# Two of three products of a split-precision matmul in one of 512 columns, in lane x's down and output projections

## The chip, the core and the metric

The kernel runs on one core of one Trainium2 chip. The metric is the time of one execution on the device in microseconds. A core has TensorE (PE in the profile; its weight loads are PEld), VectorE (DVE), ScalarE (ACT), GpSimd (POOL) and SyncE (SP), each with a queue of its own that runs in order, and DMA engines. Products land in PSUM, in eight banks of 128 partitions by 512 float32.

## The reference

Two blocks after each other, all float32, d_model 1024, 256 tokens of x and, in the second block, 256 tokens of a context. What matters is the shape of every layer of x:

```python
x = x + rms_norm(m, ln_mix_post[layer])           # m: a mixer, ends in "... @ w_out", 1024 -> 1024
h = rms_norm(x, ln_ffn_pre[layer])
x = x + rms_norm(swiglu(h, w_gate, w_up, w_down), ln_ffn_post[layer])   # w_down: 2816 -> 1024
```

x passes four mixers (pool/gating, sparse attention with retention, differential attention, grouped attention) and six feed-forward parts; so there are four output projections `@ w_out` and six down projections, each followed by an RMS norm of its result over the 1024 features. The context passes three feed-forward parts and one mixer beside it, as a second lane.

## The kernel before

Features lie on the partitions and tokens on the free axis: an activation is a stack of tiles of 128 features x 256 tokens (T = 256). Every matrix is read from HBM in blocks of 8 x 128 rows by 256 columns (1 MB; a down projection's first of three blocks has 6 x 128 rows). SP loads a block into one of four buffers `raw`, as soon as the block four before is done on TensorE.

**Three products for one.** The products must be nearly float32 but run in the faster type `f32r`. So each operand is split into an upper part, rounded to f32r, and the rest: W = whi + wlo, x = x_hi + x_lo. ACT writes whi (L223), DVE writes wlo in two halves (L230, L243). `three` (L267) then issues, for each of the k tiles of 128 inputs, whi x_hi, whi x_lo and wlo x_hi, all of 256 columns, into one half of a bank; all pass `product`, whose line is L264. Each product loads its 128x128 weights anew. `two_tiles` (L277) does a block: output tile m = 0, then m = 1; between them it emits whi and the first half of wlo for the block two or three further on (`splits`, L210), behind m = 1 the second half (`other_half`, L235). Split activations of lane x are `HNX_hi`, `HNX_lo` (8 tiles, the input of the in- and output projections) and `GX_hi`, `GX_lo` (22 tiles, the gated product, input of the down projection); each is a tensor of its own. Lane c, the context, has `HNC` and `GC`.

**Down projection** (in `ffn`, L419, lane x is the one that is not chunked): for each of four pairs of output tiles (mp), three blocks of 6, 8 and 8 k tiles, the two output tiles in two banks (`S.tiles`), of which half is used. **Output projection** (`linear`, L375, with `gain` given): four blocks, each two output tiles, two banks alike. After each pair `put_out` (L345) is emitted for the first and then the second tile: ACT reads the bank three times (L352 square, L355 square times gain, L356 copy times gain to `S.Y`), and DVE adds up (L366 and L368 the two sums of squares, L370 and L372 the product with the residual). The first tile waits for the semaphore `x_tile`, the second for the block. A bank is free for TensorE after the third ACT read.

**Behind it** `norm` (L588) sums over the partitions with small products (L538, first of `sumxy`, what L366 wrote), ACT takes the root (L525, after a table load L533), DVE inverts and spreads (L546), TensorE spreads over the partitions (L553), then DVE and ACT form the next HNX. Meanwhile TensorE gets work of lane c and of the modulation rows (L1115, L1129), as far as there is any.

**What sets the order.** All instructions are emitted by one Python program once per engine, so each engine's order is fixed. Generators for the lanes are stepped by a planner with estimated costs (`pace`, `fill`); its constants are not changed, so TensorE's order of blocks stays. Semaphore waits stand in the instruction streams: an engine waits and everything behind it waits too.

Of the kernel before, what the change touches and what calls it, by code (L numbers as in the profile page):

```python
# [9 lines left out]
P = 128  # L10
D = 1024
KD = D // P
T = 256
# [70 lines left out]
def build(nc, A, out):  # L84
# [4 lines left out]
    with ExitStack() as ctx:  # L89
        def sb(name, shape, dt=fp32):  # L90
            return ctx.enter_context(nc.sbuf_tensor(name, shape, dt))

        HX, HC = sb("HX", [P, KD, T]), sb("HC", [P, KD, T])
        WHI = [sb(f"whi{s}", [P, BLK], f32r) for s in range(HIS)]
# [5 lines left out]
        with ExitStack() as g:  # L100
            HNX = [g.enter_context(nc.sbuf_tensor(f"HNX_{n}", [P, KD, T], f32r)) for n in ("hi", "lo")]
            GX = [g.enter_context(nc.sbuf_tensor(f"GX_{n}", [P, KF, T], f32r)) for n in ("hi", "lo")]
        AX_HN, AX_G = 2 * KD * T, 2 * KF * T
# [4 lines left out]
        with ExitStack() as g:  # L108
# [21 lines left out]
        names += [f"{lane}_{n}" for lane in "xc" for n in (  # L130
            "evac", "tile", "tanh", "gate_read", "up_done", "g_hi", "g_lo", "sq", "sq_sum", "gg", "gg_sum", "hg", "hg_sum",
            "total", "root", "rstd", "scaled", "resid", "normed", "hn_hi", "hn_lo")]
# [42 lines left out]
        def program(pe=None, act=None, dve=None, pool=None, sp=None):  # L175
# [100 lines left out]

            def two_tiles(S, n, dsts, x, ks, start, stop, waits=None, signal=None, tiles=2, last=False):  # L277

                landed(n)
                for m in range(tiles):  # L280
                    mm = three(dsts[m], n, m * P, x, ks, start, stop, None if m else waits)
                    if mm is not None and m == 0 and signal is not None:
                        mm.then_inc(signal.sem, 1)
                    if m == 0:
                        splits(n, last, apart=True)
                    if m == 0 and tiles == 2:
                        opened[0] = S.tag
                        yield ("d",)
                    opened[0] = None
                other_half()  # L290
                if mm is not None:
                    mm.then_inc(sems["block_done"], 1)
# [20 lines left out]
            def halves(bank):  # L313
                return bank[:, 0:T], bank[:, T:2 * T]
# [28 lines left out]
            ALL = [(k, k) for k in range(KD)]  # L343

            def put_out(S, src, k, gain, *ready):  # L345

# [28 lines left out]
            def linear(S, name, blocks, dst, ready=(), first=None, gain=None):  # L375
# [10 lines left out]
                for j, (b, at, *alone) in enumerate(blocks):  # L386
                    tiles = 1 if alone else 2
                    if first is None or j >= 2:
                        yield ("D",)
                        n = take(S.tag, "w_main", base + b)  # L390
                        banks = (S.pair[j % 2], S.pair[j % 2])
                        dsts = halves(banks[0])
                        if gain is not None and not S.lag:
                            banks = S.tiles[2 * (j % 2)], S.tiles[2 * (j % 2) + 1]
                            dsts = banks[0][:, 0:T], banks[1][:, 0:T]
                        on(pe, *ready, *(free.get(x.name) for x in banks))
                        tile = up(f"{S.tag}_tile") if gain is not None else None
                        yield from two_tiles(S, n, dsts, S.HN, ALL, True, True, None, tile, tiles, gain is not None and j == len(blocks) - 1)
                        at_n = n
                    else:  # L400
                        banks, at_n, tile = (S.pair[j],) * 2, n + j, None

                    def job(banks=banks, at_n=at_n, at=at, tile=tile, tiles=tiles):
                        if gain is not None:
                            for m in range(2):
                                src = banks[m][:, 0:T] if not S.lag else halves(banks[m])[m]
                                free[banks[m].name] = put_out(S, src, at + m, gain, done(at_n) if m or S.lag else tile)
                            marks.append(free[banks[1].name])
                            return
# [9 lines left out]
            def ffn(S, which, gain, first):  # L419
# [6 lines left out]
                for c, pairs in enumerate(chunks):  # L426
                    for p in pairs:
# [30 lines left out]
                        def keep(p=p, nu=nu, kt=kt, down_done=down_done):  # L458
# [3 lines left out]
                            free[up_.name] = ud  # L462
                            g = [x[:, kt:kt + 2, :].rearrange("p a b -> p (a b)") for x in S.G]
                            if on(act, ud, down_done):
                                NS.activation(g[0], S.TMP[p % 2][:, :], ACT.Copy).then_inc(hi.sem, 1)  # L465
                            if on(dve, hi):
                                NV.tensor_tensor(g[1], S.TMP[p % 2][:, :], g[0].bitcast(fp32), SUB).then_inc(lo.sem, 1)
                            held[p % 2] = lo
# [6 lines left out]
                    if not S.chunked:  # L475
                        for mp in range(4):
                            banks = S.tiles[2 * (mp % 2)], S.tiles[2 * (mp % 2) + 1]
                            for cc, (k0, k1) in enumerate(SHORT_FIRST):
# [6 lines left out]
                                tile = up(f"{t}_tile") if cc == 2 else None  # L485
                                yield from two_tiles(S, n, [b[:, 0:T] for b in banks], S.G, ks, cc == 0, cc == 2, waits, tile, 2, mp == 3 and cc == 2)
                            for m in range(2):
                                free[banks[m].name] = put_out(S, banks[m][:, 0:T], 2 * mp + m, gain, done(n) if m else tile)
                        continue
# [1596 lines left out]
```

## Time and profile before

| | |
|---|---|
| time, median of 3 | 2722.41 us (2721.42 to 2722.43) |
| span of the profiled execution | 2725.8 us |
| TensorE products | 2528.6 us busy, 93% |
| TensorE weight loads | 2395.9 us, 88% |
| DVE | 1707.1 us, 63% |
| ACT | 1248.6 us, 46% |
| granted clock of TensorE | 0.97 of full speed on average |

A busy TensorE is read with care: its records overlap, so what counts is the distance from start to start. The page's slices say where it waits, the timeline what the wait was for. A mean duration is that of one record.

### The profile page before, as it was taken

What the parts mean: (1) busy time and instruction counts of PE and PEld (TensorE: products, weight loads), DVE (VectorE), ACT (ScalarE), POOL (GpSimd) and SP (SyncE); (2) the same over time, 40 slices, a digit from 0 to 9 for tenths busy, and PEclk for the clock granted to TensorE, in tenths of its full rate; (3) what the DMA queues carried; (4) which work ended last, traced back from release to release, by engine and by line L of the source; (5) the groups of instructions that cost most, each with busy time, mean ns of one, the idle gap of its engine ahead of it and who ended that gap; (6) DMA issues with size and microseconds to landing.
All of it is one profiled execution on the core that took longest, in us unless ns stands there. A gap on an engine that the chain in (4) does not pass through costs nothing.

```text
span 2725.8 us, 48854 instructions
## 1 busy us (share of the span) xinstructions
PE 2528.6 (93%) x20780; PEld 2395.9 (88%) x20780; DVE 1707.1 (63%) x2804; ACT 1248.6 (46%) x1697; POOL 1.2 (0%) x6
## 2 busy tenths in 40 slices
PE   6799997999999999999888998999999999887998
PEld 5689996888998999999887898999999999756997
DVE  6565574656766565566767576577655557646655
ACT  4443453444544444445445554455444345435443
POOL 0000000000000000000000000000000000000000
PEclk9899999999999999999898999999999999888999
DMA  6456656533555665544351344555545555363453
GB/s 218 181 200 242 241 203 229 189 109 124 186 202 216 236 226 196 211 147 154 132 174 52 120 171 154 185 175 173 179 170 179 180 177 183 114 215 137 170 178 116
DMA packets 71591, 480.14 MB, mean 176 GB/s; under 512 B 8784, under 2 KB 9296, under 8 KB 17744
## 3 DMA queue, kind: packets, MB, share of 16 engines
q1 hardware_dynamic: 66240, 468.74, 48.8%
q10 hardware_dynamic: 5136, 8.28, 1.0%
q8 instruction: 166, 2.72, 0.4%
q14 instruction: 49, 0.40, 0.0%
HBM read 471.48 MB, written 1.05 MB: 173 GB/s over the span
## 4 chain that ended last, share of the span: by engine, by line
PE 73%; DVE 13%; ACT 7%; DMA 4%; issue 3%; ACTq 0%; DVEq 0%
PE bank L264 64%; ACT whi L223 4%; DVE wlo L243 2%; DMA raw<-w_main 2%; DVE wlo L230 2%; PE bank L1115 2%; DMA raw<-w_down 1%; PE bank L997 1%; PE bank L935 1%; DVE ARX L686 1%; DVE HX L637 1%; DVE tmpx L631 1%; PE bank L985 1%; PE bank L553 0%; PE bank L1639 0%
## 5 line engine op out<-in xcount | busy, mean ns | idle before, releaser
L264 PE MATMUL bank<-HNX_hi,whi 128*128 128x256 f32 x2968 | 866.2, 293 | 64.3 <-DVE wlo L243 24.4
L223 ACT ACTIVATE whi<-raw 128x2048 fp32r<-128x2048 f32 (+1 forms) x378 | 705.5, 1868 | 334.6 <-PE bank L264 149.4
L264 PE MATMUL bank<-HNX_hi,wlo 128*128 128x256 f32 x2968 | 849.8, 287 | 0.0
L264 PE MATMUL bank<-HNX_lo,whi 128*128 128x256 f32 x2968 | 834.6, 286 | 0.0
L230 DVE TENSOR_TENSOR wlo<-raw,whi 128x1024 fp32r<-128x1024 f32 (+1 forms) x378 | 453.4, 1199 | 570.1 <-ACT whi L223 569.5
L264 PEld LDWEIGHTS bank<-HNX_hi,whi 128*128 128x128 f32 x2968 | 582.4, 196 | 91.7 <-issue 50.7
L264 PEld LDWEIGHTS bank<-HNX_hi,wlo 128*128 128x128 f32 x2968 | 583.1, 196 | 0.0
L264 PEld LDWEIGHTS bank<-HNX_lo,whi 128*128 128x128 f32 x2968 | 573.2, 196 | 1.1 <-issue 0.9
L243 DVE TENSOR_TENSOR wlo<-raw,whi 128x1024 fp32r<-128x1024 f32 (+1 forms) x378 | 450.8, 1193 | 0.0
L264 PE MATMUL bank<-HNC_hi,whi 128*128 128x256 f32 x1344 | 390.2, 290 | 11.6 <-DVE tmpc L448 4.5
L264 PE MATMUL bank<-HNC_lo,whi 128*128 128x256 f32 x1344 | 381.7, 284 | 0.0
L264 PE MATMUL bank<-HNC_hi,wlo 128*128 128x256 f32 x1344 | 381.6, 284 | 0.0
L264 PE MATMUL bank<-GX_hi,whi 128*128 128x256 f32 x1056 | 302.6, 287 | 4.0 <-DVE wlo L243 3.9
L264 PE MATMUL bank<-GX_lo,whi 128*128 128x256 f32 x1056 | 298.7, 283 | 0.0
L264 PE MATMUL bank<-GX_hi,wlo 128*128 128x256 f32 x1056 | 298.6, 283 | 0.0
L264 PEld LDWEIGHTS bank<-HNC_hi,whi 128*128 128x128 f32 x1344 | 259.2, 193 | 22.5 <-issue 7.9
L264 PEld LDWEIGHTS bank<-HNC_lo,whi 128*128 128x128 f32 x1344 | 259.4, 193 | 0.6 <-issue 0.2
L264 PEld LDWEIGHTS bank<-HNC_hi,wlo 128*128 128x128 f32 x1344 | 259.2, 193 | 0.0
L264 PEld LDWEIGHTS bank<-GX_hi,whi 128*128 128x128 f32 x1056 | 202.4, 192 | 10.4 <-DVE wlo L243 7.8
L264 PEld LDWEIGHTS bank<-GX_lo,whi 128*128 128x128 f32 x1056 | 202.5, 192 | 0.1
L264 PEld LDWEIGHTS bank<-GX_hi,wlo 128*128 128x128 f32 x1056 | 202.4, 192 | 0.0
L465 ACT ACTIVATE GX_hi<-tmpx 128x512 fp32r<-128x512 f32 x66 | 41.7, 632 | 250.0 <-DVE tmpx L461 250.0
(349 smaller groups left out, 2923.7 us busy)
## 6 DMA issues: line engine op xcount, KB each, us to landing
raw<-w_main SPq DMA_DIRECT2D x270, 1024.0 KB, 4.8
raw<-w_ada SPq DMA_DIRECT2D x72, 1024.0 KB, 4.8
raw<-w_down SPq DMA_DIRECT2D x72, 1024.0 KB, 4.9
raw<-w_down SPq DMA_DIRECT2D x36, 768.0 KB, 4.2
raw<-w_cmp SPq DMA_DIRECT2D x4, 1024.0 KB, 4.8
tmpx<-ARX ACTq DMA_DIRECT2D x18, 128.0 KB, 4.8
tmpx<-ARX ACTq DMA_DIRECT2D x32, 64.0 KB, 4.7
HX<-x_in SPq DMA_DIRECT2D x2, 512.0 KB, 6.0
```

What stands on the lines that cost most here:

```text
L223: NS.activation(WHI[q % HIS][:, 0:size], RAW[m % SLOTS][:, 0:size], ACT.Copy).then_inc(sems["w_hi"], 1)
L230: NV.tensor_tensor(WLO[m % SLOTS][:, 0:half], RAW[m % SLOTS][:, 0:half], WHI[q % HIS][:, 0:half].bitcast(fp32), SUB)
L243: NV.tensor_tensor(WLO[m % SLOTS][:, half:size], RAW[m % SLOTS][:, half:size], WHI[q % HIS][:, half:size].bitcast(fp32), SUB).then_inc(sem ...
L264: return NT.matmul(dst, (WHI[ordinal[n] % HIS], WLO[n % SLOTS])[w][:, k * 2 * P + col:k * 2 * P + col + P], x[xp][:, kx, :], start=start, ...
L465: NS.activation(g[0], S.TMP[p % 2][:, :], ACT.Copy).then_inc(hi.sem, 1)
L631: NV.tensor_tensor(S.TMP[k % 2][:, 0:T], S.Y[:, k, :], S.wide_y[:, 0:T], MUL).then_inc(sc.sem, 1)
L637: NV.tensor_tensor(S.H[:, k, :], S.H[:, k, :], S.TMP[k % 2][:, 0:T], ADD).then_inc(re.sem, 1)
L686: NV.scalar_tensor_tensor(S.Y[:, k, :], S.H[:, k, :], gain(k), S.wide_h[:, 0:T], MUL, MUL).then_inc(no.sem, 1)
L935: mm = NT.matmul(bank[:, c0 + c * T:c0 + (c + 1) * T], q[pr, :], k[pr, :], start=True, stop=True)
L985: mm = NT.transpose(turn_bank[:, c * P:(c + 1) * P], PB[w % 3][:, 0, c * P:(c + 1) * P], ident)
L997: mm = NT.matmul(out_bank[:, 0:P], v, PT[b][:, c * P:(c + 1) * P], start=c == 0, stop=c == len(vs) - 1)
L1115: mm = NT.matmul(bank[32 * g:32 * g + 32, 0:T], CCOL[:, k, 6 - 2 * r:38 - 2 * r], RAW[n % SLOTS][:, k * T:(k + 1) * T], start=r == 0 and k ...
```

## The change

In the down and output projections of lane x, `by_sides` takes the place of `three`: the upper weights are multiplied with x_hi and x_lo, which now lie side by side in one tensor (`HNX`, `GX` of shape [128, k, 2, 256]), in one product of 512 columns over a whole bank, and the lower weights with x_hi in one of 256 columns into the bank's first half. The bank then holds two partial results. A new function `both_sides` has DVE add the two halves, with a reduction over pairs, into half of `TMP[1]` (two places, by turns), and `put_out` reads from there instead of from the bank. A bank is free after that reduction. A new semaphore `x_added` orders reduction and readers; the reduction also waits until the readers of two tiles before are done. The other products of lane x (input projections, gate and up) and lane c keep three products. Where the split activations are written, the access patterns become strided over the two parts.

```diff
--- before.py
+++ after.py
@@ -90,6 +90,9 @@
         def sb(name, shape, dt=fp32):
             return ctx.enter_context(nc.sbuf_tensor(name, shape, dt))
 
+        def parts(pair):
+            return pair[:, :, 0, :], pair[:, :, 1, :], pair
+
         HX, HC = sb("HX", [P, KD, T]), sb("HC", [P, KD, T])
         WHI = [sb(f"whi{s}", [P, BLK], f32r) for s in range(HIS)]
 
@@ -98,8 +101,8 @@
         WLO = [sb(f"wlo{s}", [P, BLK], f32r) for s in range(SLOTS)]
 
         with ExitStack() as g:
-            HNX = [g.enter_context(nc.sbuf_tensor(f"HNX_{n}", [P, KD, T], f32r)) for n in ("hi", "lo")]
-            GX = [g.enter_context(nc.sbuf_tensor(f"GX_{n}", [P, KF, T], f32r)) for n in ("hi", "lo")]
+            HNX = parts(g.enter_context(nc.sbuf_tensor("HNX", [P, KD, 2, T], f32r)))
+            GX = parts(g.enter_context(nc.sbuf_tensor("GX", [P, KF, 2, T], f32r)))
         AX_HN, AX_G = 2 * KD * T, 2 * KF * T
         ARX = sb("ARX", [P, AX_HN + AX_G + KD * T])
         YX = ARX[:, AX_HN + AX_G:AX_HN + AX_G + KD * T].rearrange("p (a b) -> p a b", a=KD)
@@ -128,7 +131,7 @@
         names = ["w_in0", "w_in1", "w_in2", "w_in3", "w_hi", "w_lo", "block_done", "ada_out", "gain",
                  "in_h0", "in_h1", "in_ctx", "in_vec", "in_tab", "act_c", "pe_step", "act_step", "dve_step", "pool_step", "swapped0", "swapped1", "stored"]
         names += [f"{lane}_{n}" for lane in "xc" for n in (
-            "evac", "tile", "tanh", "gate_read", "up_done", "g_hi", "g_lo", "sq", "sq_sum", "gg", "gg_sum", "hg", "hg_sum",
+            "evac", "tile", "added", "tanh", "gate_read", "up_done", "g_hi", "g_lo", "sq", "sq_sum", "gg", "gg_sum", "hg", "hg_sum",
             "total", "root", "rstd", "scaled", "resid", "normed", "hn_hi", "hn_lo")]
         for n in names:
             sems[n] = ctx.enter_context(nc.semaphore(n))
@@ -274,11 +277,21 @@
                                          stop and j == len(ks) - 1 and w == 1)
                 return mm
 
-            def two_tiles(S, n, dsts, x, ks, start, stop, waits=None, signal=None, tiles=2, last=False):
+            def by_sides(bank, n, col, x, ks, start, stop, waits=None):
+
+                mm = None
+                for j, (k, kx) in enumerate(ks):
+                    if on(pe, *(waits or {}).get(kx, ())):
+                        NT.matmul(bank[:, :], WHI[ordinal[n] % HIS][:, k * 2 * P + col:k * 2 * P + col + P],
+                                  x[2][:, kx, :, :].rearrange("p a b -> p (a b)"), start=start and j == 0, stop=False)
+                        mm = product(bank[:, 0:T], n, col, k, x, 0, kx, 1, False, stop and j == len(ks) - 1)
+                return mm
+
+            def two_tiles(S, n, dsts, x, ks, start, stop, waits=None, signal=None, tiles=2, last=False, sides=False):
 
                 landed(n)
                 for m in range(tiles):
-                    mm = three(dsts[m], n, m * P, x, ks, start, stop, None if m else waits)
+                    mm = (by_sides if sides else three)(dsts[m], n, m * P, x, ks, start, stop, None if m else waits)
                     if mm is not None and m == 0 and signal is not None:
                         mm.then_inc(signal.sem, 1)
                     if m == 0:
@@ -341,6 +354,15 @@
                 splits(n + 1)
 
             ALL = [(k, k) for k in range(KD)]
+
+            def both_sides(S, bank, k, *ready):
+
+                at = k % 2 * T
+                added = up(f"{S.tag}_added")
+                if on(dve, *ready, free.get((S.tag, "added", k % 2))):
+                    NV.tensor_reduce(S.TMP[1][:, at:at + T], bank[:, :].rearrange("p (s t) -> p t s", s=2), AX, ADD).then_inc(added.sem, 1)
+                free[bank.name] = added
+                return S.TMP[1][:, at:at + T], added
 
             def put_out(S, src, k, gain, *ready):
 
@@ -391,11 +413,11 @@
                         banks = (S.pair[j % 2], S.pair[j % 2])
                         dsts = halves(banks[0])
                         if gain is not None and not S.lag:
-                            banks = S.tiles[2 * (j % 2)], S.tiles[2 * (j % 2) + 1]
-                            dsts = banks[0][:, 0:T], banks[1][:, 0:T]
+                            dsts = banks = S.tiles[2 * (j % 2)], S.tiles[2 * (j % 2) + 1]
                         on(pe, *ready, *(free.get(x.name) for x in banks))
                         tile = up(f"{S.tag}_tile") if gain is not None else None
-                        yield from two_tiles(S, n, dsts, S.HN, ALL, True, True, None, tile, tiles, gain is not None and j == len(blocks) - 1)
+                        yield from two_tiles(S, n, dsts, S.HN, ALL, True, True, None, tile, tiles, gain is not None and j == len(blocks) - 1,
+                                             gain is not None and not S.lag)
                         at_n = n
                     else:
                         banks, at_n, tile = (S.pair[j],) * 2, n + j, None
@@ -403,9 +425,12 @@
                     def job(banks=banks, at_n=at_n, at=at, tile=tile, tiles=tiles):
                         if gain is not None:
                             for m in range(2):
-                                src = banks[m][:, 0:T] if not S.lag else halves(banks[m])[m]
-                                free[banks[m].name] = put_out(S, src, at + m, gain, done(at_n) if m or S.lag else tile)
-                            marks.append(free[banks[1].name])
+                                if S.lag:
+                                    free[banks[m].name] = ev = put_out(S, halves(banks[m])[m], at + m, gain, done(at_n))
+                                    continue
+                                src, added = both_sides(S, banks[m], at + m, done(at_n) if m else tile)
+                                free[S.tag, "added", m] = ev = put_out(S, src, at + m, gain, added)
+                            marks.append(ev)
                             return
                         ev = up(f"{S.tag}_evac")
                         if on(act, done(at_n), *free.get((S.tag, "dst"), ())):
@@ -460,11 +485,11 @@
                             if on(dve, done(nu), held["read", p % 2]):
                                 NV.scalar_tensor_tensor(S.TMP[p % 2][:, :], S.TMP[p % 2][:, :], 0.5, up_[:, :], MUL, MUL).then_inc(ud.sem, 1)
                             free[up_.name] = ud
-                            g = [x[:, kt:kt + 2, :].rearrange("p a b -> p (a b)") for x in S.G]
+                            g, both = [x[:, kt:kt + 2, :] for x in S.G[:2]], S.TMP[p % 2][:, :].rearrange("p (a b) -> p a b", a=2)
                             if on(act, ud, down_done):
-                                NS.activation(g[0], S.TMP[p % 2][:, :], ACT.Copy).then_inc(hi.sem, 1)
+                                NS.activation(g[0], both, ACT.Copy).then_inc(hi.sem, 1)
                             if on(dve, hi):
-                                NV.tensor_tensor(g[1], S.TMP[p % 2][:, :], g[0].bitcast(fp32), SUB).then_inc(lo.sem, 1)
+                                NV.tensor_tensor(g[1], both, g[0].bitcast(fp32), SUB).then_inc(lo.sem, 1)
                             held[p % 2] = lo
                             lo_marks[kt // 2] = lo
                         after(S, keep)
@@ -483,9 +508,10 @@
                                 ks = [(k - k0, k) for k in range(k0, k1)]
                                 waits = {k: [lo_marks[k // 2]] for k in range(k0, k1) if k % 2 == 0} if mp == 0 else None
                                 tile = up(f"{t}_tile") if cc == 2 else None
-                                yield from two_tiles(S, n, [b[:, 0:T] for b in banks], S.G, ks, cc == 0, cc == 2, waits, tile, 2, mp == 3 and cc == 2)
+                                yield from two_tiles(S, n, banks, S.G, ks, cc == 0, cc == 2, waits, tile, 2, mp == 3 and cc == 2, True)
                             for m in range(2):
-                                free[banks[m].name] = put_out(S, banks[m][:, 0:T], 2 * mp + m, gain, done(n) if m else tile)
+                                src, added = both_sides(S, banks[m], 2 * mp + m, done(n) if m else tile)
+                                free[t, "added", m] = put_out(S, src, 2 * mp + m, gain, added)
                         continue
                     k0, k1 = CHUNKS[c]
                     for mp in range(4):
```

## Rows read from the trace of the kernel before

**Rows 1.** The page, parts 1 and 4: busy time by engine, and the chain by line.
```profile
PE 2528.6 (93%) x20780; PEld 2395.9 (88%) x20780; DVE 1707.1 (63%) x2804; ACT 1248.6 (46%) x1697; POOL 1.2 (0%) x6
...
PE bank L264 64%; ACT whi L223 4%; DVE wlo L243 2%; DMA raw<-w_main 2%; DVE wlo L230 2%; PE bank L1115 2%; DMA raw<-w_down 1%; PE bank L997 1%; PE bank L935 1%; DVE ARX L686 1%; DVE HX L637 1%; DVE tmpx L631 1%; PE bank L985 1%; PE bank L553 0%; PE bank L1639 0%
```

**Rows 2.** Groups, part 5: busy us, mean ns, idle before.
```profile
L264 PE MATMUL bank<-GX_hi,whi 128*128 128x256 f32 x1056 | 302.6, 287 | 4.0 <-DVE wlo L243 3.9
```

**Rows 3.** Timeline, TensorE, full clock: start us, duration us, instruction, count.
```profile
355.15 0.28 PE L264 MATMUL bank<-GX_hi,whi 128*128 128x256 f32 x1
355.27 0.28 PE L264 MATMUL bank<-GX_lo,whi 128*128 128x256 f32 x1
```

**Rows 4.** Timeline, TensorE, half clock.
```profile
1312.26 0.41 PE L264 MATMUL bank<-HNX_hi,whi 128*128 128x256 f32 x1
1312.47 0.41 PE L264 MATMUL bank<-HNX_hi,wlo 128*128 128x256 f32 x1
```

**Rows 5.** Timeline, TensorE, full clock, float32; first row is the second's first record.
```profile
673.34 0.59 PE L818 MATMUL bank<-tmpx,VEC 128*128 128x512 f32 x1
673.34 1.02 PE L818 MATMUL bank<-tmpx,VEC 128*128 128x512 f32 x2
...
1448.01 0.27 PE L985 MATMUL bank<-VEC,ARX 128*128 128x128 f32 x1
1448.12 0.61 PE L997 MATMUL bank<-ARX 128*128 128x128 f32 x4
```

**Rows 6.** Groups of DVE, shapes apart.
```profile
L961 DVE TENSOR_REDUCE SMALL<-bank 128x1 f32<-128x512 f32 x48 | 31.5, 685 | 15.5 <-PE bank L935 15.5
...
L1436 DVE TENSOR_TENSOR ARX<-ARX 64x480 f32<-64x480 f32 x4 | 3.9, 963 | 1.0 <-PE bank L1448 0.9
...
L575 DVE TENSOR_REDUCE diagx<-ARX 128x256 f32<-128x1024 f32 x1 | 1.9, 1880 | 0.0
```

**Rows 7.** Timeline, ACT, output projection of the last mixer.
```profile
2485.84 1.92 ACT L223 ACTIVATE whi<-raw 128x2048 fp32r<-128x2048 f32 x1
...
2491.79 0.38 ACT L352 ACTIVATE sqx<-bank 128x256 f32<-128x256 f32 x1 [1.77 <-PE bank L264]
...
2492.43 0.48 ACT L356 ACTIVATE ARX<-bank,GA 128x256 f32<-128x256 f32 x1
...
2499.06 1.92 ACT L223 ACTIVATE whi<-raw 128x2048 fp32r<-128x2048 f32 x1
```

**Rows 8.** Timeline, DVE, ends of two output projections.
```profile
713.79 0.42 DVE L366 TENSOR_TENSOR sumxy<-sumxy,sqx 128x256 f32<-128x256 f32 x1
...
2506.50 0.42 DVE L366 TENSOR_TENSOR sumxy<-sumxy,sqx 128x256 f32<-128x256 f32 x1
...
2507.96 0.42 DVE L366 TENSOR_TENSOR sumxy<-sumxy,sqx 128x256 f32<-128x256 f32 x1
```

**Rows 9.** Timeline, TensorE, first total at stage ends; bracket: idle before, releaser.
```profile
364.60 0.32 PE L538 MATMUL bank<-sumxy,VEC 128*32 128x64 f32 x8
...
718.80 0.32 PE L538 MATMUL bank<-sumxy,VEC 128*32 128x64 f32 x8
...
1302.74 0.44 PE L538 MATMUL bank<-sumxy,VEC 128*32 128x64 f32 x8 [3.47 <-DVE sumxy L366]
...
2315.67 0.32 PE L538 MATMUL bank<-sumxy,VEC 128*32 128x64 f32 x8 [1.25 <-DVE sumxy L366]
...
2508.43 0.44 PE L538 MATMUL bank<-sumxy,VEC 128*32 128x64 f32 x8 [3.63 <-DVE sumxy L366]
...
2712.73 0.32 PE L538 MATMUL bank<-sumxy,VEC 128*32 128x64 f32 x8 [1.25 <-DVE sumxy L366]
```

**Rows 10.** Timeline, ACT, after the first output projection.
```profile
118.46 1.28 ACT L533 ACT_TABLE_LOAD   x1
...
122.09 1.91 ACT L223 ACTIVATE whi<-raw 128x2048 fp32r<-128x2048 f32 x1 [2.13 <-DMA raw<-w_main]
123.90 0.30 ACT L525 ACTIVATE sqx<-bank,VEC 128x64 f32<-128x64 f32 x1
```

## The prediction

> **What bounds the kernel now.** I read the page's totals and chain first. TensorE is busy 93% of the span and one line, the split-precision product L264, is 64% of the chain that ended last [rows 1]. So a nanosecond off a product is a real nanosecond wherever TensorE streams without a gap. The grouped view then gives the part touched: 1056 products of each kind on GX [rows 2], and by the loops another 4 x 8 x 8 = 256 on HNX in the four output projections: 1312 triples. The timeline of TensorE shows their pitch: one product every 0.120 us at full clock [rows 3]. Last I read what TensorE waits for where a stage ends: L538 adds up the sums of `put_out`, and there the reader should look at the brackets [rows 9]. In five of the ten stage ends of x it comes without a wait, after work of lane c; in the other five something of the sums or the ACT queue behind them comes last. In those, TensorE's speed does not set the end; the DVE/ACT chain does.
>
> **The triple.** Old cost 3 x 0.120 = 0.360 us. New: one product of 512 columns and one of 256; as many columns, one weight load fewer. The second keeps 0.120. What the first costs no row shows. At half clock the same 256-column product has a pitch of 0.21 us [rows 4], which is 256/1.2 GHz = 0.213 with nothing on top; at full clock 0.120 stands against 256/2.4 = 0.107, so 0.013 us is on top. Three readings. (a) The load limits it and hides under a longer stream: the float32 records of 512 columns, at two clocks per column, come 1.02 - 0.59 = 0.43 apart = 2 x 0.213 with no excess [rows 5], so 0.213 + 0.120 = 0.333, say 0.336. (b) It is a cost of each product: 0.227 + 0.120 = 0.347. (c) It is a limit of the rate at which this type streams, and the half clock hides it: 0.240 + 0.120 = 0.360, no gain. Against (a): with a fresh load of 128 columns each, float32 records of 128 columns (as many clocks, at two per column) keep a pitch of (0.61 - 0.27)/3 = 0.113 [rows 5], so a load need not take 0.120. I take (b), between the ends and nearest to the row of the product itself: 0.013 saved per triple, 2.35 us in a down projection (176 triples), 0.85 in an output projection (64), 17.5 us in all, if nothing else intervened. The ends are 31.5 us and 0.
>
> The Trainium skill, TensorE: Matmul & The Clock Gate, section Back-to-back issue gap, gives a warm gap of N/2.4 + 2.5 ns: 216 ns for 512 columns, which is reading (a). By that rule the total above would be 31.5 us; but the same rule gives 109 ns for 256 columns and the trace shows 120, so it misses just the term in dispute.
>
> **The added reduction.** 80 times (10 stages x 8 tiles) DVE reads 512 elements of a bank in pairs 256 apart and writes 256. A contiguous reduction of 512 from a bank takes 0.685 us; two operations on SBUF that step over elements are dearer, 1.880 us for 1024 and 0.963 for 480 [rows 6], a slope of 0.917/544 = 1.69 ns per element and 0.15 fixed. That gives 0.15 + 512 x 0.00169 = 1.02 us. Ends: 0.69 (a bank does not mind the step) and 1.4 (if the cost were per output of the reduction). I take 1.02, the row with the same access order. DVE as a whole has room; the total of 80 us is not the price.
>
> The Trainium skill speaks against this edit: SBUF — State Buffer, section Door 1: The DMA port swizzle, says PSUM lines hold two FP32 values and non-contiguous patterns cost; VectorE: DVE Perf Modes, in its table of TRN2 errata, has 120 + FD cycles for a bank source, 0.66 us here, 0.36 less than my term. The sum by it would be some 8 us lower.
>
> **The added order.** This costs more. Before, ACT read the bank directly, so it ran its three operations of tile k+1 (1.12 us from start to end, [rows 7]) while DVE still added those of tile k; DVE needs 1.46 us per tile [rows 8] (from one last L366 to the next). Now DVE must reduce tile k+1 before ACT may start, and that reduction stands in DVE's queue behind the four adds of tile k, of which the last two wait for ACT. So DVE holds 1.02 + 1.12 + 0.9 (two adds) = 3.05 us per tile, 1.6 more. Behind it in DVE's queue are the halves of wlo; behind ACT's part is the next whi (1.92 us, [rows 7]).
> In a down projection a pair of tiles has three weight blocks (15 us of TensorE) for 6.1 us of this and 6.5 us of wlo: hidden. In an output projection each pair has one block: whi 1.9, wlo 2.35 (two halves of 1.2), first tile 3.05, second until ACT is free 2.1, together 9.4 us per block against 5.5 us of TensorE. Now the whi of two blocks apart come at 2485.84 and 2499.06, 6.6 per block [rows 7]. Blocks are split two ahead, so TensorE is not held inside; the lag comes out at the end.
>
> **Stage by stage, against the profiled execution.**
> - Output projection ending at 2508.43 (nothing covers it, TensorE already waits 3.63 us on L366 [rows 9]): whi slips from 2499.06 [rows 7] to 2506.0 (1.4 in the first block, 2.8 in each of two); then whi 1.9, a short copy of ACT 0.4, second whi 1.9, wlo 2.35, put_out of both tiles to the last L366 3.05 + 1.91 = 11.5, so 2517.5: **+9.1**.
> - The one ending at 118.54: there ACT's L525 comes only at 123.90, since a whi before it waits for its DMA until 122.09 [rows 10]; that is 5 us of cover. The last ACT operation of put_out now ends where the table load L533 starts, at 118.46 [rows 10]; the lag puts it 6.3 later (about 1 after the first block, 2.8 after each of the next two, nothing in the last, which splits no block), to 124.8; then table load 1.3, whi 1.9 and L525 at 128.0: **+4.1**.
> - The one ending at 718.80: L366 ends at 714.21 [rows 8] and TensorE comes 4.6 us later [rows 9]. The lag, with two whi in the last block as at 2508, is 9.1 again and brings L366 to 723.3: **+4.5**. The third output projection (at 1631) has lane c between its blocks, so the lag is smaller, and it too is covered: **-0.9**.
> - Down projections at 364.60 and two like it, where TensorE comes without a wait [rows 9] and the chain is 3.1 longer: **-2.35 each, -7.0**.
> - At 1302.74, waiting 3.47 us [rows 9], with wlo just before: 3.05 - 2.35 = **+0.7**. At 2315.67: the first tile's reduction waits for wlo, the last L366 comes 2.4 later: **0**. At 2712.73: 1.25 later: **-1.1**.
>
> Sum +9.3 us. Banks come free earlier or as before (the reduction ends before the old third ACT read). The strided writes to HNX/GX and the fewer instructions I take at nothing: same element counts. 2725.8 of span stands for a median of 2722.4, 3.4 more; 2735.1 of span is **2731.7 us**.
>
> **Rivals.**
> - *Load hidden, cheap reduction (faster).* Reading (a) and 0.69 us: (a) gives back 12 us more where TensorE sets the pace (6 x 1.9 + 0.7), the cheaper reduction 8 us in the exposed ends (6 to 8 of them in a row at 118, 718 and 2508). 2731.7 - 20 = 2711.5. For: no excess in the 0.43 row. Against: the 0.113 row and both stepping rows. Chance 0.20.
> - *Load hidden, reduction at 1.02:* 2731.7 - 12 = 2719.7, within 0.2%. Chance 0.21.
> - *Rate limit (slower).* Reading (c): the six down projections gain nothing, 15 us more: 2746.7. For: half clock hides the excess wholly, as a rate limit would. It decides from a 512-column pitch of 0.235 up. Chance 0.24.
> - *The change does what it says and DVE's order costs more* (splits of lane c late behind x's longer chain at 718 and after): 5 to 10 us on top of any case; I have no row for it, it widens the upper end.
> - *Forecast:* 0.35, own range 2724 to 2741, of which the lower tenth is within 0.2%.
>
> 0.2% is 5.4 us, about what a measurement can tell from no change. Faster 0.21 (the first rival and an edge), same 0.26, slower 0.53. The range leaves out half of the first rival and the worst of the third with late splits: 2710 to 2750.
>
> **What would show it.** Right: L264 on GX with 128x512 at a pitch near 0.227; reductions near 1.0 us; L538 at the ends of both uncovered output projections waiting 8 us and more on DVE's L366, whi blocks 9 us apart in them; the down projections about 2.3 us shorter. Wrong: a pitch of 0.215 or 0.24; a reduction near 0.7; output projections whose last L366 keeps its distance to the last product, which would mean that I misread the order of DVE's queue.

## The result and the profile after

The changed kernel takes 2781.22 us (median of 4, 2779.68 to 2789.38) where the kernel before takes 2722.42 on the same chip; ratio 1.0232, interval 1.0219 to 1.0244. It is slower by 59 us, and the forecast was 2731.7, at most 2750. The profiled execution has a span of 2787.3 us, 61.5 more than that of before; the table below accounts for those. It is the slowest of the four executions.

The page of the changed kernel, parts 1 and 5 (busy us, share, count; then groups: busy us, mean ns, idle before and its releasers):

```profile
PE 2538.4 (91%) x19468; PEld 2337.1 (84%) x19468; DVE 1766.9 (63%) x2884; ACT 1255.0 (45%) x1697; POOL 1.2 (0%) x6
...
L285 PE MATMUL bank<-GX,whi 128*128 128x512 f32 x1056 | 385.7, 407 | 14.0 <-DVE wlo L246 14.0
...
L363 DVE TENSOR_REDUCE tmpx<-bank 128x256 f32<-128x512 f32 x80 | 54.8, 685 | 15.6 <-PE bank L267 15.6
```

The busy shares have hardly moved against [rows 1]. The reduction took 0.685 us, as the contiguous one of [rows 6] does. The first totals of lane x's stage ends, for [rows 9] (timeline of TensorE; the bracket is its idle time and who ended it):

```profile
125.32 0.44 PE L564 MATMUL bank<-sumxy,VEC 128*32 128x64 f32 x8 [3.23 <-DVE sumxy L388]
370.90 0.32 PE L564 MATMUL bank<-sumxy,VEC 128*32 128x64 f32 x8
738.07 0.32 PE L564 MATMUL bank<-sumxy,VEC 128*32 128x64 f32 x8
1026.40 0.32 PE L564 MATMUL bank<-sumxy,VEC 128*32 128x64 f32 x8
1340.52 0.44 PE L564 MATMUL bank<-sumxy,VEC 128*32 128x64 f32 x8 [6.37 <-DVE sumxy L388]
1668.01 0.32 PE L564 MATMUL bank<-sumxy,VEC 128*32 128x64 f32 x8
1994.73 0.32 PE L564 MATMUL bank<-sumxy,VEC 128*32 128x64 f32 x8
2371.32 0.44 PE L564 MATMUL bank<-sumxy,VEC 128*32 128x64 f32 x8 [3.23 <-DVE sumxy L388]
2570.10 0.44 PE L564 MATMUL bank<-sumxy,VEC 128*32 128x64 f32 x8 [8.45 <-DVE sumxy L388]
2774.28 0.32 PE L564 MATMUL bank<-sumxy,VEC 128*32 128x64 f32 x8 [2.07 <-DVE sumxy L388]
```

Set against the same marks before, how much longer each stretch up to its mark became:

| mark before | what ends there | forecast | measured |
|---|---|---|---|
| 118.54 | output projection | +4.1 | +6.8 |
| 364.60 | down projection | -2.35 | -0.5 |
| 718.80 | output projection | +4.5 | +13.0 |
| 1008.21 | down projection | -2.35 | -1.1 |
| 1302.74 | down projection | +0.7 | +19.6 |
| 1630.95 | output projection | -0.9 | -0.7 |
| 1947.08 | down projection | -2.35 | +10.6 |
| 2315.67 | down projection | 0 | +8.0 |
| 2508.43 | output projection | +9.1 | +6.0 |
| 2712.73 | down projection | -1.1 | -0.1 |

Four stretches (718, 1302, 1947, 2315) hold 51 of the 61 us. The two that I had called certain losses at their ends (118 and 2508) make 12.8 where 13.2 was forecast. All the brackets of TensorE's timeline together are 187.0 us before and 239.3 after: 52.3 us of new waiting. The pitch gives some 9 back (below), so by difference about 18 us are left for running at the lower clock. The timeline gives the same when it is counted: at the lower clock the distances from start to start exceed those of the same shapes at full clock by 59.7 us in all before and by 79.0 after. The mean granted clock fell from 0.966 to 0.956. Here TensorE comes back from 3.00 us of waiting at 1.2 GHz, with a pitch of 0.21 us like that of [rows 4], and keeps it for 5.8 us.

```profile
377.65 0.58 PE L267 MATMUL bank<-HNC_hi,whi 128*128 128x256 f32 x1 [3.00 <-DVE tmpc L473]
378.03 0.42 PE L267 MATMUL bank<-HNC_lo,whi 128*128 128x256 f32 x1
378.25 0.42 PE L267 MATMUL bank<-HNC_hi,wlo 128*128 128x256 f32 x1
```

That block of lane c began 3.1 us later, counted from the stage end before it, and finished another 2.4 later. So this wait cost more than its bracket.

**Where the 19.6 us come from.** Between the blocks of the down projection at 1302, lane c computes its attention: small products, read by ACT (L1058, now L1084), and TensorE's next small product waits for that read. First a place in the kernel before, ACT and then DVE (timeline):

```profile
1240.05 0.39 ACT L352 ACTIVATE sumxy<-bank 128x256 f32<-128x256 f32 x1
...
1242.00 1.98 ACT L223 ACTIVATE whi<-raw 128x2048 fp32r<-128x2048 f32 x1
1243.81 0.44 ACT L1058 ACTIVATE ARC<-bank 128x256 f32<-128x256 f32 x1
```
```profile
1240.69 0.49 DVE L1050 SCALAR_TENSOR_TENSOR ARC<-ARC,SMALL 128x256 f32<-128x256 f32 x1
1241.09 1.22 DVE L243 TENSOR_TENSOR wlo<-raw,whi 128x1024 fp32r<-128x1024 f32 x1
1242.22 0.42 DVE L361 TENSOR_TENSOR sumxg<-HX,ARX 128x256 f32<-128x256 f32 x1
```

The same place in the changed kernel, DVE, ACT, and TensorE behind them:

```profile
1261.20 1.22 DVE L246 TENSOR_TENSOR wlo<-raw,whi 128x1024 fp32r<-128x1024 f32 x1
1262.33 0.68 DVE L363 TENSOR_REDUCE tmpx<-bank 128x256 f32<-128x512 f32 x1
1264.30 0.42 DVE L383 TENSOR_TENSOR sumxg<-HX,ARX 128x256 f32<-128x256 f32 x1 [1.28 <-ACT ARX L378]
1264.64 0.68 DVE L363 TENSOR_REDUCE tmpx<-bank 128x256 f32<-128x512 f32 x1
1265.81 0.43 DVE L388 TENSOR_TENSOR sumxy<-sumxy,sqx 128x256 f32<-128x256 f32 x1 [0.48 <-ACT sqx L374]
```
```profile
1263.05 0.42 ACT L374 ACTIVATE sumxy<-tmpx 128x256 f32<-128x256 f32 x1 [2.78 <-DVE tmpx L363]
...
1265.36 0.42 ACT L374 ACTIVATE sqx<-tmpx 128x256 f32<-128x256 f32 x1 [1.09 <-DVE tmpx L363]
...
1266.48 1.89 ACT L226 ACTIVATE whi<-raw 128x2048 fp32r<-128x2048 f32 x1
1268.28 0.36 ACT L1084 ACTIVATE ARC<-bank 128x256 f32<-128x256 f32 x1
```
```profile
1269.00 1.23 PE L1045 MATMUL bank<-KC,ARC 64*128 64x256 f32 x4 [3.77 <-ACT ARC L1084]
```

Before, ACT began its six reads of the banks at 1240.05, before DVE had even come to the half of wlo (1241.09). Now it begins only behind that half and a reduction. From the start of the same half of wlo, ACT's first read went from 1.04 us ahead to 1.85 behind, that is 2.9 us; and from that first read to whi it takes 3.43 us instead of 1.95, since ACT waits 1.09 for the second reduction, which stands behind DVE's 1.28 for ACT. Both together put the read L1084 4.4 us later against that half of wlo, and TensorE waits 3.77 for it, where the timeline of before shows no wait. DVE isn't full: it waits too. Two engines with room hand each tile to and fro, and a third one waits behind both. The same wait comes again at 1294.3 and 1318.6, with brackets of 4.32 and 4.29. The group of these small products, before and then changed:

```profile
L1019 PE MATMUL bank<-KC,ARC 64*128 64x256 f32 x64 | 11.2, 426 | 4.3 <-ACT ARC L1058 4.3
```
```profile
L1045 PE MATMUL bank<-KC,ARC 64*128 64x256 f32 x64 | 11.8, 444 | 14.7 <-ACT ARC L1084 14.7
```

Of the 15.5 us of new brackets in this stretch that is 10.4; the wait at its end holds another 2.9 (6.37 against 3.47).

**The stretches to 1947 and 2315 have another wait.** These small products stand in the stretch to 1302 alone. In the other two, lane c's norm and the split weights come late behind x's chain. TensorE, before and then changed: the largest wait inside x's down projection in the stretch to 1947, then that for lane c's norm in the stretch to 2315.

```profile
1899.38 0.38 PE L264 MATMUL bank<-GX_hi,whi 128*128 128x256 f32 x1 [0.77 <-DVE wlo L243]
2304.66 0.48 PE L553 MATMUL bank<-tmpc,VEC 128*128 128x256 f32 x1 [0.31 <-DVE tmpc L546]
```
```profile
1945.16 0.80 PE L285 MATMUL bank<-GX,whi 128*128 128x512 f32 x1 [4.12 <-DVE wlo L246]
2357.18 0.79 PE L579 MATMUL bank<-tmpc,VEC 128*128 128x256 f32 x1 [2.76 <-DVE tmpc L572]
```

Over the whole kernel the waits of TensorE for wlo are the largest part of the 52.3 us, 20.6 of them (waits of TensorE, before and then changed: us in total, times, longest):

```profile
PE bank L264 <- DVE wlo L243: 28.6, 24, 3.5
```
```profile
PE bank L267 <- DVE wlo L246: 30.0, 19, 4.2
...
PE bank L285 <- DVE wlo L246: 19.2, 14, 4.1
```

### The profile page after: what moved, and what is told of

It reads as the page before. It is cut to its first block, busy times and chain, and to the rows that moved or that the text cites. A ratio compares the mean times of both kernels' runs of the same rounds, so it can differ in the third digit from the quotient of the medians.

```text
span 2787.3 us, 46388 instructions
## 1 busy us (share of the span) xinstructions
PE 2538.4 (91%) x19468; PEld 2337.1 (84%) x19468; DVE 1766.9 (63%) x2884; ACT 1255.0 (45%) x1697; POOL 1.2 (0%) x6
## 4 chain that ended last, share of the span: by engine, by line
PE 64%; DVE 17%; ACT 10%; issue 4%; DMA 4%; ACTq 0%; DVEq 0%
PE bank L267 50%; PE bank L285 6%; ACT whi L226 5%; DVE wlo L246 3%; DMA raw<-w_main 3%; DVE wlo L233 3%; PE bank L1141 2%; DVE tmpx L363 1%; PE bank L1023 1%; ACT diagx L377 1%; PE bank L961 1%; ACT ARX L378 1%; DMA raw<-w_down 1%; DVE ARX L712 1%; DVE HX L663 1%
## 5 line engine op out<-in xcount | busy, mean ns | idle before, releaser
L267 PE MATMUL bank<-HNX,whi 128*128 128x256 f32 x5424 | 1023.9, 290 | 63.3 <-DVE wlo L246 25.6
L267 PEld LDWEIGHTS bank<-HNX,whi 128*128 128x128 f32 x5424 | 868.3, 196 | 89.3 <-issue 48.3
L267 PE MATMUL bank<-HNX,wlo 128*128 128x256 f32 x2968 | 848.7, 287 | 0.0
L267 PEld LDWEIGHTS bank<-HNX,wlo 128*128 128x128 f32 x2968 | 582.0, 196 | 0.0
L285 PE MATMUL bank<-GX,whi 128*128 128x512 f32 x1056 | 385.7, 407 | 14.0 <-DVE wlo L246 14.0
L267 PE MATMUL bank<-GX,wlo 128*128 128x256 f32 x1056 | 299.1, 283 | 0.0
L285 PEld LDWEIGHTS bank<-GX,whi 128*128 128x128 f32 x1056 | 202.3, 192 | 68.6 <-DVE wlo L246 18.2
L267 PEld LDWEIGHTS bank<-GX,wlo 128*128 128x128 f32 x1056 | 203.2, 192 | 0.1
L267 PE MATMUL bank<-GC_hi,whi 128*128 128x256 f32 x528 | 155.1, 294 | 4.3 <-DVE wlo L246 4.3
L267 PE MATMUL bank<-GC_lo,whi 128*128 128x256 f32 x528 | 150.9, 286 | 0.0
```

The source lines that it names most:

```text
L267: return NT.matmul(dst, (WHI[ordinal[n] % HIS], WLO[n % SLOTS])[w][:, k * 2 * P + col:k * 2 * P + col + P], x[xp][:, kx, :], start=start, ...
L285: NT.matmul(bank[:, :], WHI[ordinal[n] % HIS][:, k * 2 * P + col:k * 2 * P + col + P], x[2][:, kx, :, :].rearrange("p a b -> p (a b)"), st ...
```

## The experiments

The kernel before ran in the same rounds; times are medians, and ratios are to it. Three theories: A, the passing of each tile between DVE and ACT; B, DVE's added work; C, the wide product or what belongs to it.

**Without the addition.**
```diff
-src, added = both_sides(S, banks[m], 2 * mp + m, done(n) if m else tile)
-free[t, "added", m] = put_out(S, src, 2 * mp + m, gain, added)
+free[banks[m].name] = put_out(S, banks[m][:, 0:T], 2 * mp + m, gain, done(n) if m else tile)
```


> The products as changed, but no reduction: put_out reads the first side of the bank with ACT as before; whi x_lo is computed and not added in the four output and six down projections, so the result lacks that part. Theory A (order): the loss comes from DVE and ACT having to pass each tile to and fro; the products themselves gain 1312 x (0.360 - 0.353) = 9.2 us: 2713 us. Theory B (DVE time): the 80 x 0.685 = 55 us of reductions crowd DVE; also 2713. Theory C (product): the 512-column product, the full bank or the strided split activations cost elsewhere; then it stays near the changed kernel, 2770 or more.


Measured 2712.69 against 2719.85, ratio 0.9977 (0.9967 to 0.9987). C falls: wide products, full banks and strided activations are no loss but a gain of some 7 us (3.5 to 9.0 by the interval), a little under the pitch's 9.2. The brackets of TensorE are 187.8 us, as before the change (187.0): the new waiting comes with the addition.

**Narrow products, with the addition.**
```diff
-NT.matmul(bank[:, :], WHI[...], x[2][:, kx, :, :]..., start=start and j == 0, stop=False)
+product(bank[:, 0:T], n, col, k, x, 0, kx, 0, start and j == 0, False, True)
+product(bank[:, T:2 * T], n, col, k, x, 1, kx, 0, False, False, True)
```


> Two sides and the reduction, but three products of 256 columns as before (whi x_lo goes to the second side on its own). A and B: the changed kernel's time plus the 9.2 us that the pitch of 0.353 gave: 2790 us. C: the loss goes with the wide product, 2725 to 2740.


Measured 2787.43, ratio 1.0249 (1.0234 to 1.0263). The whole loss comes without a single wide product.

**A reduction that nobody reads.** DVE reduces 512 elements of HX at the same places, 680 ns each, and `put_out` reads the bank.
```diff
-NV.tensor_reduce(S.TMP[1][:, at:at + T], bank[:, :].rearrange("p (s t) -> p t s", s=2), AX, ADD).then_inc(added.sem, 1)
+NV.tensor_reduce(S.TMP[1][:, at:at + T], S.H[:, 0:2, :].rearrange("p a b -> p (a b)").rearrange("p (t s) -> p t s", s=2), AX, ADD)
```


> As the first, and a reduction of 512 to 256 elements stands in DVE's queue at the same places behind the same waits on TensorE, but reads the residual stream and nobody waits for it; ACT reads the bank directly. The result lacks whi x_lo as there. Theory A: DVE has room, and what costs is that ACT waits for DVE; so most of the loss is gone, 2713 plus 0.7 to 1.4 in each of the five uncovered stage ends, some 2720 (2714 to 2730). Theory B: nearly the whole loss is there, 2765 to 2785.


Measured 2722.97, ratio 1.0007 (0.9997 to 1.0016): 10 us above the kernel without addition (8 by the ratios). B alone is worth that, of the 68 us (69 by the ratios) that lie between the kernel without addition and the changed one.

**A wait without a reduction.**
```diff
+NV.tensor_reduce(S.TMP[1][:, at:at + 1], S.H[:, 0, 0:2], AX, ADD).then_inc(added.sem, 1)
+gate = both_sides(S, 2 * mp + m, done(n) if m else tile)
+free[banks[m].name] = free[t, "added", m] = put_out(S, banks[m][:, 0:T], 2 * mp + m, gain, gate)
```


> In the changed kernel's order, but in place of the reduction DVE does one element (two numbers of the residual stream into one, a cost of next to nothing), for which ACT waits before it reads the first side of the bank itself; the sum with whi x_lo is left out. It prices the waits alone. Theory A (the passing to and fro): of the 68 us between the kernel without addition (2713) and the changed one (2781) more than half stays without any reduction: 2748 to 2765. Rival (the reduction's own 0.69 us, in DVE's queue and in the chain, is the price): 2715 to 2730.


Measured 2745.64, ratio 1.0085 (1.0066 to 1.0103). The operation it adds takes 0.15 us (DVE, groups):

```profile
L362 DVE TENSOR_REDUCE tmpx<-HX 128x1 f32<-128x2 f32 x80 | 11.9, 149 | 23.7 <-PE bank L267 23.7
```

33 of the 68 us (29 of 69 by the ratios), slightly below the range of A and far above the rival's: ACT standing behind DVE's queue costs three times what the reductions cost as work. Work alone 10, wait alone 33, both 68: the other 25 to 32 come only together. I have not split these further, and their cause stays open. One reason may be that the reduction's own time now stands in the chain twice per pair. Another may be that ACT's three reads take longer from `TMP` than from the bank: 1.12 us from tile to tile (1241.83 to 1242.95 below) against 0.97 before (1240.05 to 1241.02).

**Both reductions ahead of both `put_out`.**
```diff
+sums = [both_sides(S, banks[m], 2 * mp + m, done(n) if m else tile) for m in range(2)]
 for m in range(2):
-    src, added = both_sides(S, banks[m], 2 * mp + m, done(n) if m else tile)
-    free[t, "added", m] = put_out(S, src, 2 * mp + m, gain, added)
+    free[t, "added", m] = put_out(S, sums[m][0], 2 * mp + m, gain, sums[m][1])
```


> The changed kernel with the two reductions of a pair of tiles emitted ahead of both put_out. Theory A: worked from the changed kernel's timeline (reductions 0.69, three reads of ACT 1.2, four adds 1.46), ACT is then held about 3.1 us per pair instead of 4.0 to 4.7 and DVE 4.4 instead of 5.6, so a third to a half of the 60 us goes: 2750 us (2740 to 2762). Theory B: DVE's work is the same, 2778 to 2783.


Measured 2748.74, ratio 1.0100 (1.0085 to 1.0115): the same operations in another order are 32 us cheaper (36 by the ratios). At the place above ACT now runs its six reads in one go:

```profile
1241.83 0.42 ACT L374 ACTIVATE sumxy<-tmpx 128x256 f32<-128x256 f32 x1 [2.78 <-DVE tmpx L363]
1242.15 0.49 ACT L377 ACTIVATE sumxh<-tmpx,GA 128x256 f32<-128x256 f32 x1
1242.55 0.49 ACT L378 ACTIVATE ARX<-tmpx,GA 128x256 f32<-128x256 f32 x1
1242.95 0.40 ACT L374 ACTIVATE sqx<-tmpx 128x256 f32<-128x256 f32 x1
```

2.23 us from the first read to whi (at 1244.06) instead of 3.43; the 2.78 of waiting behind wlo and a reduction stay. TensorE's brackets fell from 239.3 to 204.1.

**The first reduction ahead of the half of wlo as well.** `two_tiles` calls `both_sides` for tile 0 before `other_half()`.


> Both reductions ahead of both put_out, and the first of them ahead of the second half of wlo, as soon as the first tile is done, so that ACT's first three reads run beside wlo. Theory A: another part of what is left (2749 against 2713 + 10 for DVE's time) goes: 2740 (2733 to 2745). Rival: the halves of wlo now wait behind a reduction that waits for TensorE, and the split weights come late: 2750 to 2765.


Measured 2744.86, ratio 1.0083 (1.0064 to 1.0103). The wait at this place fell from 2.78 to 1.64, but the time against the run before isn't told apart from no change; other blocks got their wlo later, as TensorE's waits for it show, 39.4 us instead of 33.8.

**GpSimd takes two of the four additions.** With both reductions ahead, the product with the residual and its sum are issued by `eng, N = (dve, NV) if S.lag else (pool, NG)`, GpSimd for lane x; DVE's first scaling behind the norm also waits for GpSimd's last sum.


> Both reductions of a pair ahead of both put_out, and GpSimd, which is idle, takes the product with the residual and its sum (two of DVE's four additions per tile) in lane x's put_out. Theory A with a small share for DVE's time (the unread reduction cost some 10 us): DVE gets 0.75 us per tile back, 2748 - 10 to 15 = 2735 us. Rival: GpSimd is slower than DVE at this and its last sum comes late at the stage ends, or the two engines hinder each other: 2748 or more.


Measured 2750.44, ratio 1.0104 (1.0081 to 1.0128): nothing won. Groups of GpSimd and DVE:

```profile
L395 POOL TENSOR_TENSOR sumxg<-sumxg,tmpx 128x256 f32<-128x256 f32 x70 | 54.9, 785 | 5.5
L393 POOL TENSOR_TENSOR tmpx<-HX,ARX 128x256 f32<-128x256 f32 x70 | 52.4, 748 | 2587.2 <-ACT ARX L378 2584.0 <-POOL sumxg L395 0.5
```
```profile
L390 DVE TENSOR_TENSOR sumxh<-sumxh,diagx 128x256 f32<-128x256 f32 x70 | 42.3, 605 | 1.7 <-ACT diagx L377 1.7
...
L390 DVE TENSOR_TENSOR sumch<-sumch,tmpc 128x256 f32<-128x256 f32 x28 | 11.8, 421 | 0.0
```

DVE's addition of lane x, beside which GpSimd works, takes 605 ns (420 in the kernel with both ahead); the same line for lane c, whose sums GpSimd has no part in, keeps 421.

**Only in down projections, only in output projections** (order as changed).


> Sides and reduction in the six down projections alone; the output projections keep three products, order as in the changed kernel. From the lag of TensorE's stream of the changed kernel behind the one before: about 23 us of the 61 are gained in and right behind the four output projections (4.6, 6.5, 5 and 7.4), 38 in the down projections and what lane c does between their blocks. Theory A1 (the places are independent): 2722 + 37 = 2759 us. Rival A2 (what one place loses another absorbs, or the losses pull each other up): clearly off that, and the two partial kernels together don't make 59 us. My step-by-step reading, in which down projections hide the chain, would give 2715 to 2722.

> Sides and reduction in the four output projections alone. A1: 2722 + 22 = 2744 us. A2: clearly off that. The reading of the prediction, in which nearly all of the loss is here, would give 2735 to 2780.


Measured 2761.49, ratio 1.0155 (1.0140 to 1.0170), and 2745.12, ratio 1.0093 (1.0076 to 1.0110). 41 and 25 us make 66, where both at once cost 59: the places add up but for a tenth, and the larger part lies where I had forecast a gain. In the first of these the stretch up to 1302.74 alone is 18.0 us longer, that up to 2315.67 10.0.

**Only three down projections**, the ones without attention of lane c between their blocks, with the first reduction ahead of the half of wlo.


> The order of the run before this one, with sides only in the down projections in which the lane of the context does no attention between the blocks (the first, second and sixth), where the kernel with sides in all six lost at most a microsecond. Pitch gives 3 x 176 x 0.0075 = 4.0 us, the chain at the ends takes 1 to 2: 2718 to 2721 where before is 2720; at best just inside what can be measured. Rival (DVE's extra work costs everywhere): 2725.


Measured 2728.02, ratio 1.0022 (1.0011 to 1.0033): the rival. Even there the addition costs more than the 4 us of pitch; where, no trace shows. None of the complete versions run here beats the kernel before.

**The pitch.** First the lower product is left out of `by_sides`, so that wide follows wide.


> The product with the lower weights is left out in by_sides, so that products of 512 columns follow each other: it measures the pitch that was in dispute. (a) load hides: 0.216 us; (b) a cost per product: 0.227; (c) a rate at which the columns stream: 0.240, as the pairs of the changed kernel (0.353 in all) suggest. The time falls by up to 1312 x 0.113 = 148 us, less where DVE and ACT set the pace: 2640 to 2680 us.


The single execution took 2736.87 us. With 132 us of busy TensorE less than the changed kernel it gained 44 only; the brackets of TensorE rose from 239.3 to 318.9. Then the kernel without addition, with a second loop over `ks` for the narrow products behind the loop of the wide ones.


> The kernel without the addition (first run), with one more edit: a tile's wide products come first, then its narrow ones, instead of wide and narrow by turns. In the trace wide after wide stood 0.227 to 0.231 us apart in the run with the upper product alone, narrow after narrow 0.120, and a mixed pair takes 0.3525. If the turns of shape cost those 0.006 us (reading b is right for each shape by itself), it gains 1312 x 0.006 = 8 us: 2705 against 2713. If a pair costs 0.353 in any order, 2713.


Measured 2707.97, ratio 0.9956 (0.9943 to 0.9970), some 5 us less than by turns where 8 were expected, with intervals that just overlap; the pitches show it more surely. TensorE's timeline: the changed kernel, then the last run.

```profile
2749.78 0.40 PE L285 MATMUL bank<-GX,whi 128*128 128x512 f32 x1
2750.02 0.28 PE L267 MATMUL bank<-GX,wlo 128*128 128x256 f32 x1
2750.13 0.40 PE L285 MATMUL bank<-GX,whi 128*128 128x512 f32 x1
...
2753.31 0.40 PE L285 MATMUL bank<-GX,whi 128*128 128x512 f32 x1
```
```profile
2677.38 2.00 PE L285 MATMUL bank<-GX,whi 128*128 128x512 f32 x8
2679.22 1.12 PE L267 MATMUL bank<-GX,wlo 128*128 128x256 f32 x8
2680.17 2.00 PE L285 MATMUL bank<-GX,whi 128*128 128x512 f32 x8
```

By turns ten pairs take 2753.31 - 2749.78 = 3.53, so 0.353 each. By shape, eight pairs take 2.79, so 0.349; inside a row wide products stand (2.00 - 0.40)/7 = 0.229 apart, narrow ones (1.12 - 0.28)/7 = 0.120.

## Why the prediction was wrong

- **The triple.** Reading (b), 0.347, was nearly right for each shape by itself (0.229 + 0.120 = 0.349), but not for the alternation: 0.353. The term was 0.013 per triple and measured 0.007, some 9 us instead of 17.5. The run without addition gained 7. I had no term for a change of shape.
- **The reduction.** 1.02 forecast, 0.685 measured: the lower end was right, and the stepping operations on SBUF were the wrong row. My slope ran through two unlike operations, an addition and a reduction of four. Memory alone isn't the difference: the reduction of neighbours on SBUF that nobody reads took 680 ns; no run has pairs 256 apart on SBUF. The Trainium skill (VectorE: DVE Perf Modes, table of TRN2 errata) has 120 + FD cycles, 0.66 us as an estimate, and the trace agrees within 4%. The sentence of the Trainium skill that non-contiguous patterns in PSUM cost (SBUF — State Buffer, Door 1: The DMA port swizzle), which I had set against this edit, speaks of matmuls. It isn't borne out for DVE: pairs 256 apart took 685 ns, like 512 contiguous elements.
- **The added order at the output projections.** Blocks 9.4 us apart were forecast; the second reductions of the last one's blocks start at 2539.3, 2548.2 and 2557.0, so 8.8 to 8.9, less by the cheaper reduction. L564 waits 8.45 us at 2570, "8 us and more" as written. The order in DVE's queue was read rightly. That the two uncovered ends make 12.8 us for 13.2 is partly luck: the stretch to 118 lost 6.8 for 4.1, that to 2508 6.0 for 9.1. "TensorE is not held inside" was wrong: it waits for wlo within these projections, 1.66 us at 115.21, 1.91 at 718.98 and 1.66 at 2554.43.
- **"Hidden" in a down projection: the step that failed.** I compared 6.1 + 6.5 us of DVE with 15 us of TensorE per pair, as if only the total counted and only x's stage end waited for this chain. But ACT's and DVE's queues also carry lane c between the blocks, and TensorE's own order is fixed, so that in the middle of x's down projection it waits for what stands behind `put_out`: for the read L1084 in the stretch to 1302, for wlo and lane c's norm in those to 1947 and 2315. I had named "whi" as what stands behind ACT's part, and not the read of lane c behind that. The stretches 1302, 1947 and 2315 were forecast at -1.7 together and measured at +38.2; 29 us of that are brackets of TensorE (15.5, 5.8 and 7.8). The kernel with sides in the down projections alone loses 41 us.
- **The covered stage ends.** For 718 I counted only the end, +4.5; there TensorE waits 1.91 and 2.93 us for wlo, at 718.98 and 727.79. But 5.5 of the 13 us came at the beginning of the stretch: at 377.65 lane c waits for `tmpc` (L473). ACT's two whi behind the down projection's chain began 3.72 us ahead of the mark before (360.88) and only 0.25 ahead of it now (370.65), and ACT's and then DVE's work on `tmpc` stands behind them. What was covered at one mark was paid at the next wait.
- **The clock.** I had no term for it: 18 us by difference, 19.3 when counted.
- The rival "DVE's order costs more", 5 to 10 us with the words "I have no row for it", was the right mechanism, sized far too small. A row existed for its largest place: the group L1019 of the kernel before, with its 4.3 us of idle time behind ACT's L1058, says that TensorE already waits there now and then, so that a later read of ACT is soon paid.

## What to carry to other kernels

An operation put between two engines isn't priced by its duration alone but by whose queue it stands in: ask what stands ahead of it there, what the engine behind it had done in the meantime before, and who waits for that engine's next operations, in every lane that shares the queues. If it has to be there, emit it for all tiles ahead of the work that depends on it; the same operations in that order cost 32 us less here. A term for a wait on TensorE needs a second term for the products that then run at 1.2 GHz: here 52.3 us of new waits came with some 18 us of slower products.

## What the runs showed of the hardware

- Products of 512 columns of this type have a pitch of 0.229 us in a row, ones of 256 columns 0.120; by turns a pair takes 0.353 instead of 0.349. Grouping them by shape gained some 5 us.
- A reduction over pairs 256 apart in a PSUM bank costs as much as a contiguous one, 685 ns for 512 elements.
- GpSimd took 748 to 785 ns for 128x256 float32 where DVE takes 420, and DVE's addition beside it went from 420 to 605 ns.
- After a wait of 3.00 us TensorE ran at 1.2 GHz for 5.8 us, with a pitch of 0.21 us instead of 0.12.
